# The delta rule's beta and alpha projection: which operand is stationary, in a two-block mixer kernel

## The chip, the cores and the metric

The kernel runs on one NeuronCore of a Trainium2 chip. The metric is the device time of one execution in microseconds; the figure given for a kernel is the median of several executions. TensorE (PE in the profile) multiplies; its weight loads are shown apart as PEld. VectorE is DVE, ScalarE is ACT, GpSimd is POOL, and SP issues the DMAs.

## The reference, cut to what matters

Two blocks of two layers each run over 256 tokens of width 1024. In each layer of the first block one input projection feeds a delta rule and a Hyena branch. Sixteen of its columns are the delta rule's beta logits and alpha:

```
proj = _rmsnorm(x, mix_norm[i]) @ w_in[i]
q, k, v, z, beta_logit, alpha, hy_in = jnp.split(proj, IN_SPLITS, axis=-1)
...
beta = jax.nn.sigmoid(beta_logit...)          # 8 columns: 2 directions x 4 heads
g = -jnp.exp(a_log) * jax.nn.softplus(alpha + dt_bias)   # 8 columns
o_fwd = _gated_delta_rule(q, k, v, beta[0], g[0])
```

So for these the kernel needs a 256 x 1024 by 1024 x 16 product in each of two layers. The kernel uses it with tokens on the partitions: two blocks of 128 tokens (`rb`), 16 columns each, 32 columns in all, in `small[:, 304:336]`.

## The kernel before

All weights of the two blocks are streamed from HBM in the order of use. SP loads 1 MB units into `raw`; ACT rounds each half (128 x 1024) to `w_hi` (L568), POOL takes the rest as `w_lo` (L949), and PE uses the pair. Each matrix product is three matmuls, in `product` (lines 412 to 414): low by high, high by low, high by high. There are four slots for halves; ACT works three halves ahead of PE.

`project_T(0, l, 66 + i, psA[:, i % 3, 0:L])` makes one block of 128 output channels by 256 tokens: over 8 blocks of the 1024 inputs (`kc`) it loads 128 x 128 weights as the stationary operand and moves `xT` (128 x 256), 24 matmuls in all. The text calls it project(i). In `stack1_projections` PE runs i from 0 to 27: 0 to 11 are Hyena's channels, 12 to 23 are q, k and v, and 24 to 27 are z. ACT takes each result out of PSUM (L719 for q, k, v), DVE adds the other four taps of the short convolution (`convolve1`, L1168, conv(i)), and ACT applies silu. Before project(i) PE waits for conv(i - 3), whose PSUM bank it takes. Between these steps stand, by a fixed list of i in each engine's own program, other pieces: on PE after i = 16 `gate_columns`, the product for beta and alpha, and after i = 22 `qk_sums`. On DVE, after conv(17), the 32 columns are copied to `small` (L1219); after conv(19) come the inverse root of the Hyena norm (L962 to L974) and the scaling of `zz` (L1225), after conv(20) the sums with alpha (L1230, L1232) which ACT turns into exponentials (L740) at i = 22.

In `gate_columns` the stationary operand is a 128 x 128 block of `xT`, and the 16 weight columns move: 2 blocks of tokens x 8 `kc` x 3 = 48 matmuls in a layer, each 128 x 16. In the profile's rows a matmul's names are given as output<-moving,stationary, so these read `psA<-wba_hi,xT_lo 128x16`, and those of project(i) read `psA<-xT_hi,w_lo 128x256`.

Each engine runs its own instructions strictly in the order written; semaphores of the table `s1` (`ba_mm`, `ba_out`, `conv`, and others) hold one engine for another.

Of the kernel before, what the change touches and what calls it, by code (L numbers as in the profile page):

```python
# [31 lines left out]
P = 128  # L32
D = 1024
L = 256
RB = L // P
KC = D // P
# [139 lines left out]
def emit(nc, ins, out, count):  # L176

    steps = {}
    with ExitStack() as ctx:
# [3 lines left out]
        def sb(name, shape, dt=F32):  # L183
            return ctx.enter_context(nc.sbuf_tensor(name, shape, dt))

        def psum(name, shape):
            return ctx.enter_context(nc.psum_tensor(name, shape, F32))
# [6 lines left out]
        xT_hi = sb("xT_hi", [P, KC, L], F32R)  # L194
        xT_lo = sb("xT_lo", [P, KC, L], F32R)
# [11 lines left out]
        small = sb("small", [P, 400])  # L207
        root_mix = sb("root_mix", [P, 2, L])
        ident, ones, blockones = mats[:, 0, :], mats[:, 1, :], mats[:, 2, :]
# [18 lines left out]
        def at(name, kb, shape, dt=F32):  # L228
            n = 4 * int(np.prod(shape[1:]))
            assert kb * KB + n <= ARENA, name  # L230
            return nc.alloc_sbuf_tensor_at(name, shape, dt, offset=at0 + int(kb * KB))
# [28 lines left out]
        hdn = at("hdn", 105.0, [HID, L + 1])  # L260
        farg = at("farg", 102.0, [HID, 2, L])
        skip = at("skip", 83, [P, 2, HYW])
        zz = at("zz", 103, [P, RB, HYW])
        knat = at("knat", 75, [P, RB, HEADS, P])
        vnat = at("vnat", 79, [P, RB, HEADS, P])
# [24 lines left out]
        wba_hi = at("wba_hi", 62, [P, KC, 16], F32R)  # L290
        wba_lo = at("wba_lo", 62.5, [P, KC, 16], F32R)
# [29 lines left out]
        psA = psum("psA", [P, 4, 512])  # L321
# [49 lines left out]
        def one_stack(per):  # L371
            return {k: Signal(sem(k), n) for k, n in per.items()}

        NPAR1, NPAR2 = 20, 14
        s1 = one_stack(dict(
            cols_tp=1, cols=1, wba=1, mlp_mm=3, mlp_arg=3, mlp_sin=3, filt_mm=8, filt=8, even=4, odd=4, spec_mm=10, spec=10,
            conv_mid=24, conv=24, qkv_silu=12, z_out=4, z_silu=1, ba_mm=1, ba_out=1, hy_turned=6, hy_nat=6,
            z_mm=8, y_spec=4, inv_mm=4, zz=4, hy_ss=2, hy_zn=1, hy_back=2, y_hi=6, y_lo=6,
            qk_sq=1, qk_mm=1, qk_root=1, qk_norm=1, kv_turned=4, kv_nat=4,
            g_arg=1, g_exp=1, g_sum=1, g_ln=1, g_ready=1, g_cum=1, g_col=1, g_decays=1,  # L380
            row_mm=4, row_arg=4, row_exp=4, q_exp=2, q_dec=2, kk_mm=1, attn=4, mt=5,
            masked=24, p_mm=28, q_new=24, t_new=4, u_new=4, tu_mm=20, tu_copy=24,
            v1_mm=2, v1=2, k_dec=2, s_mm=2, s_copy=2, ks_mm=2, rest=2, v2_mm=2, v2=2, o_mm=2,
# [26 lines left out]
        def product(o, a_hi, a_lo, b_hi, b_lo, start, stop, skip=False):  # L410

            nc.tensor.matmul(o, a_lo, b_hi, start=start, stop=False, skip_group_check=skip)  # L412
            nc.tensor.matmul(o, a_hi, b_lo, start=False, stop=False, skip_group_check=skip)  # L413
            return nc.tensor.matmul(o, a_hi, b_hi, start=False, stop=stop, skip_group_check=skip)  # L414
# [541 lines left out]
        def _(dve):  # L956
            V = nc.vector
# [249 lines left out]
            def stack1_projections(l):  # L1207
                ch = dve_chain[0]
                for i in range(24):
                    convolve1(l, i)  # L1210
                    if i in (10, 13):
                        spectral_product(l, i // 13, 0)
                        spectral_product(l, i // 13, 1)
                    if i in (12, 15):
                        hyena_gate(l, i // 15, 0)
                        hyena_gate(l, i // 15, 1)
                    if i == 17:
                        dve.wait_ge(s1["ba_mm"].sem, s1["ba_mm"].due(l, 1))
                        V.tensor_copy(small[:, 304:336], psA[:, 3, 0:32]).then_inc(s1["ba_out"].sem, 1)  # L1219
                        dve.wait_ge(s1["ba_out"].sem, s1["ba_out"].due(l, 1))  # L1220
                    if i == 19:
                        dve.wait_ge(s1["hy_ss"].sem, s1["hy_ss"].due(l, 2))
                        inverse_root(l, ch, small[:, 292:294], small[:, 288:290], 1.0 / HYW)
                        for rb in range(RB):
                            ins_ = V.tensor_scalar(zz[:, rb, :], zz[:, rb, :], small[:, 292 + rb:293 + rb], None, ALU.mult)  # L1225
                        ins_.then_inc(s1["hy_zn"].sem, 1)
                    if i == 20:
                        for rb in range(RB):
                            alpha = small[:, 312 + 16 * rb:320 + 16 * rb]
                            V.tensor_tensor(small[:, 16 + 8 * rb:24 + 8 * rb], alpha, small[:, 8:16], ALU.add).then_inc(ch.sem, 1)  # L1230
                            dve.wait_ge(ch.sem, ch.step(l))
                        V.scalar_tensor_tensor(small[:, 32:48], small[:, 16:32], -1.0, small[:, 16:32], ALU.mult, ALU.max)\  # L1232
                            .then_inc(s1["g_arg"].sem, 1)
# [318 lines left out]
            for col, value in ((eps, EPS), (eps64, 64 * EPS), (eps128, 128 * EPS), (stat[:, 3:4], D * EPS * EPS)):  # L1552
                ins_ = V.memset(col, value)
# [43 lines left out]
        def _(pe):  # L1597
# [31 lines left out]
            def project_T(st, l, s, o, q=None):  # L1629

                pe.wait_ge(lo_done[st].sem, lo_done[st].due(l, s + 1))
                hi, lo = split_half(w_hi, s, "A"), split_half(w_lo, s, "A")
                for kc in range(KC):
                    if q is not None and kc % 2 == 0:
                        pe.wait_ge(n_lo[st].sem, n_lo[st].due(l, 4 * q + kc // 2 + 1))
                    ins_ = product(o, hi[:, kc, :], lo[:, kc, :], xT_hi[:, kc, :], xT_lo[:, kc, :], kc == 0, kc == KC - 1)
                ins_.then_inc(half_used[st].sem, 1)
# [128 lines left out]
            def gate_columns(l):  # L1766

                pe.wait_ge(s1["wba"].sem, s1["wba"].due(l, 1))
                pe.wait_ge(s1["hy_nat"].sem, s1["hy_nat"].due(l, 6))
                for rb in range(RB):  # L1770
                    t = slice(rb * P, (rb + 1) * P)
                    for kc in range(KC):
                        ins_ = product(psA[:, 3, 16 * rb:16 * rb + 16], xT_hi[:, kc, t], xT_lo[:, kc, t],
                                       wba_hi[:, kc, :], wba_lo[:, kc, :], kc == 0, kc == KC - 1)
                ins_.then_inc(s1["ba_mm"].sem, 1)

            def qk_sums(l):
# [7 lines left out]
            def stack1_projections(l):  # L1785

                for i in range(28):
                    if 3 <= i < 27:
                        pe.wait_ge(s1["conv"].sem, s1["conv"].due(l, i - 2))
                    elif i == 27:  # L1790
                        pe.wait_ge(s1["z_out"].sem, s1["z_out"].due(l, 1))
                    project_T(0, l, 66 + i, psA[:, i % 3, 0:L], 1 if i == 0 else None)
                    if i == 5:
                        turn_hyena(l, 0)
                        turn_hyena(l, 1)
                    if i == 9:
                        turn_hyena(l, 2)
                        turn_hyena(l, 3)
                    if i == 10:
                        hyena_spectrum(l, 0)  # L1800
                    if i == 12:
                        hyena_inverse(l, 0)
                    if i == 13:
                        hyena_spectrum(l, 1)
                        turn_hyena(l, 4)
                    if i == 14:
                        turn_hyena(l, 5)
                    if i == 15:
                        hyena_inverse(l, 1)
                    if i == 16:  # L1810
                        gate_columns(l)
                    if i == 22:
                        qk_sums(l)
                pe.wait_ge(s1["hy_zn"].sem, s1["hy_zn"].due(l, 1))
                pe.wait_ge(s1["z_out"].sem, s1["z_out"].due(l, 2))
                pe.wait_ge(s1["ba_out"].sem, s1["ba_out"].due(l, 1))
                for b in range(4):
                    for rb in range(RB):
                        c = (b % 2) * L + rb * P
                        ins_ = nc.tensor.transpose(psA[:, 1 + b // 2 * 2, c:c + P], zz[:, rb, b * P:(b + 1) * P], ident)  # L1820
                    if b % 2:
                        ins_.then_inc(s1["hy_back"].sem, 1)
# [318 lines left out]
```

## Time and profile before

| | |
|---|---|
| median of 3 runs | 2204.73 us (2200.49 to 2206.77) |
| the profiled execution: its own time | 2204.25 us |
| its span in the trace | 2202.4 us |
| PE matmul busy | 2082.2 us, 95% |
| DVE, ACT, POOL busy | 974.9, 1033.1, 1496.3 us |
| mean granted TensorE clock | 0.977 of full |

A busy PE is an engine with a matmul under way, whatever clock it was granted and however few columns it moves. The granted clock is given as a share of full speed in the column PEclk of a table by stretches: 1.00 is 2.4 GHz and 0.50 is 1.2 GHz, and a value between them means that the stretch holds some of each. For the pace of a stream of matmuls the distance between two starts is to be read, not the duration of one, since they overlap.

### The profile page before, as it was taken

What the parts mean: (1) busy time and instruction counts of PE and PEld (TensorE: products, weight loads), DVE (VectorE), ACT (ScalarE), POOL (GpSimd) and SP (SyncE); (2) the same over time, 40 slices, a digit from 0 to 9 for tenths busy, and PEclk for the clock granted to TensorE, in tenths of its full rate; (3) what the DMA queues carried; (4) which work ended last, traced back from release to release, by engine and by line L of the source; (5) the groups of instructions that cost most, each with busy time, mean ns of one, the idle gap of its engine ahead of it and who ended that gap; (6) DMA issues with size and microseconds to landing.
All of it is one profiled execution on the core that took longest, in us unless ns stands there. A gap on an engine that the chain in (4) does not pass through costs nothing.

```text
span 2202.4 us, 37209 instructions
## 1 busy us (share of the span) xinstructions
PE 2082.2 (95%) x15887; PEld 1895.2 (86%) x15887; DVE 974.9 (44%) x1647; ACT 1033.1 (47%) x1532; POOL 1496.3 (68%) x656
## 2 busy tenths in 40 slices
PE   7999998899999999998899999889999998889999
PEld 6997768879989997778889988888899888888997
DVE  3550475524204551366533204555477026454760
ACT  5443426355446443516364436346644363366442
POOL 6788434238887887424258887657688866577886
PEclk9999998899999999998999999999999999999999
DMA  6756222025555655323025564444455544444553
GB/s 227 219 182 199 85 88 97 21 63 187 191 185 168 217 183 178 104 70 115 3 94 176 191 223 148 153 126 156 150 174 189 196 135 154 131 157 154 180 185 133
DMA packets 250397, 329.63 MB, mean 150 GB/s; under 512 B 9016, under 2 KB 224954, under 8 KB 249722
## 3 DMA queue, kind: packets, MB, share of 16 engines
q1 hardware_dynamic: 249834, 325.15, 45.7%
q8 instruction: 126, 2.06, 0.4%
q0 software_dynamic: 400, 2.10, 0.2%
q14 instruction: 37, 0.30, 0.0%
HBM read 326.18 MB, written 1.05 MB: 149 GB/s over the span
## 4 chain that ended last, share of the span: by engine, by line
PE 53%; DVE 6%; ACT 3%; POOL 2%; issue 1%; DVEq 0%; ACTq 0%
PE psA L412 11%; PE psA L413 10%; PE psA L414 10%; PE psB L412 5%; PE psB L413 5%; PE psB L414 5%; POOL w_lo L949 2%; PE psA L1733 1%; PE psB L1756 1%; PE psB L1763 1%; ACT w_hi L568 1%; DVE yacc L1536 0%; PE psA L1889 0%; PE psA L1891 0%; PE psB L1879 0%
## 5 line engine op out<-in xcount | busy, mean ns | idle before, releaser
L949 POOL TENSOR_TENSOR w_lo<-raw,w_hi 128x1024 fp32r<-128x1024 f32 x600 | 1461.9, 2454 | 634.2 <-ACT w_hi L568 631.8
L412 PE MATMUL psA<-xT_hi,w_lo 128*128 128x256 f32 x3296 | 955.3, 290 | 53.0 <-DVE xT_lo L999 15.4
L413 PE MATMUL psA<-xT_lo,w_hi 128*128 128x256 f32 x3296 | 941.2, 286 | 0.0
L414 PE MATMUL psA<-xT_hi,w_hi 128*128 128x256 f32 x3296 | 940.7, 285 | 0.0
L568 ACT ACTIVATE w_hi<-raw 128x1024 fp32r<-128x1024 f32 x600 | 628.8, 1051 | 409.6 <-PE psB L414 249.1
L412 PEld LDWEIGHTS psA<-xT_hi,w_lo 128*128 128x128 f32 x3296 | 641.2, 195 | 67.2 <-issue 25.9
L413 PEld LDWEIGHTS psA<-xT_lo,w_hi 128*128 128x128 f32 x3296 | 641.5, 195 | 3.0 <-issue 2.9
L414 PEld LDWEIGHTS psA<-xT_hi,w_hi 128*128 128x128 f32 x3296 | 641.2, 195 | 0.0
L1097 DVE TENSOR_TENSOR hT_lo<-hfull,hT_hi 128x256 fp32r<-128x256 f32 x132 | 220.4, 1701 | 2.3 <-ACT hT_hi L688 1.3
L413 PE MATMUL psB<-w_lo,hT_hi 128*128 128x512 f32 x528 | 209.5, 397 | 0.0
L412 PE MATMUL psB<-w_hi,hT_lo 128*128 128x512 f32 x528 | 209.0, 396 | 0.4 <-issue 0.4
L414 PE MATMUL psB<-w_hi,hT_hi 128*128 128x512 f32 x528 | 207.4, 393 | 0.0
L1041 DVE SCALAR_TENSOR_TENSOR x<-psB,stat,x 128x512 f32<-128x512 f32 x24 | 17.1, 752 | 336.5 <-PE psB L414 336.5
L1093 DVE TENSOR_TENSOR hfull<-sg,psA 128x256 f32<-128x256 f32 x132 | 55.0, 420 | 232.0 <-PE psA L414 219.0
L412 PEld LDWEIGHTS psB<-w_hi,hT_lo 128*128 128x128 f32 x528 | 99.1, 188 | 25.2 <-issue 0.8
L414 PEld LDWEIGHTS psB<-w_hi,hT_hi 128*128 128x128 f32 x528 | 99.1, 188 | 24.6
L413 PEld LDWEIGHTS psB<-w_lo,hT_hi 128*128 128x128 f32 x528 | 99.1, 188 | 22.7
L688 ACT ACTIVATE hT_hi<-hfull 128x256 fp32r<-128x256 f32 x132 | 54.4, 414 | 118.9 <-DVE hfull L1093 118.8
L679 ACT ACTIVATE sg<-gs 128x256 f32<-128x256 f32 x88 | 36.0, 413 | 147.3 <-DVE gs L1073 147.3
L1073 DVE TENSOR_TENSOR gs<-psA,root_row 128x256 f32<-128x256 f32 x88 | 35.8, 419 | 102.2 <-PE psA L414 73.6
L682 ACT ACTIVATE sg<-gconv 128x256 f32<-128x256 f32 x44 | 18.4, 417 | 100.9 <-DVE gconv L1060 100.9
L1168 DVE SCALAR_TENSOR_TENSOR qkvT<-psA,cols,qkvT 128x254 f32<-128x254 f32 (+1 forms) x96 | 46.1, 482 | 40.3 <-ACT qkvT L719 37.7
(415 smaller groups left out, 2257.6 us busy)
## 6 DMA issues: line engine op xcount, KB each, us to landing
raw<-in_w_in SPq DMA_DIRECT2D x78, 1024.0 KB, 5.3
raw<-in_ffn_w_gate SPq DMA_DIRECT2D x44, 1024.0 KB, 5.3
raw<-in_ffn_w_up SPq DMA_DIRECT2D x44, 1024.0 KB, 5.4
raw<-in_ffn_w_down SPq DMA_DIRECT2D x44, 1024.0 KB, 4.9
raw<-in_w_ffn_in SPq DMA_DIRECT2D x44, 1024.0 KB, 5.1
raw<-in_w_ffn_out SPq DMA_DIRECT2D x22, 1024.0 KB, 4.8
raw<-in_w_out SPq DMA_DIRECT2D x16, 1024.0 KB, 4.9
raw<-in_w_branch_da SPq DMA_DIRECT2D x4, 1024.0 KB, 4.9
```

The lines of the kernel that those rows point to most:

```text
L412: nc.tensor.matmul(o, a_lo, b_hi, start=start, stop=False, skip_group_check=skip)
L413: nc.tensor.matmul(o, a_hi, b_lo, start=False, stop=False, skip_group_check=skip)
L414: return nc.tensor.matmul(o, a_hi, b_hi, start=False, stop=stop, skip_group_check=skip)
L568: A(split_half(w_hi, n, kinds[n]), raw_half(n, kinds[n]), ACT.Copy).then_inc(hi_done[st].sem, 1)
L679: A(sg[:, i, :], gs[:, i, :], ACT.Silu).then_inc(f_act[st].sem, 1)
L688: A(hT_hi[:, n, :], hfull[:, i, :], ACT.Copy).then_inc(f_hi[st].sem, 1)
L949: nc.gpsimd.tensor_tensor(split_half(w_lo, n, kind), raw_half(n, kind), split_half(w_hi, n, kind).bitcast(F32), ALU.subtract)\
L1073: V.tensor_tensor(gs[:, i, :], psA[:, i, 0:L], root_row[:, :], ALU.mult).then_inc(f_gate[st].sem, 1)
L1093: V.tensor_tensor(hfull[:, i, :], sg[:, i, :], psA[:, 2 + i, 0:L], ALU.mult).then_inc(f_prod[st].sem, 1)
L1097: V.tensor_tensor(hT_lo[:, n, :], hfull[:, i, :], hT_hi[:, n, :].bitcast(F32), ALU.subtract)\
L1168: ins_ = V.scalar_tensor_tensor(o[:, a:z], ps[:, a + t:z + t], w[t + len(w) // 2], o[:, a:z], ALU.mult, ALU.add)
L1733: ins_ = M(psA[:, k % 4, :], dft_f[:, rb, b, :], src, start=(rb == 0), stop=(rb == RB - 1))
```

## The change

The operands of the product for beta and alpha change places. The 16 weight columns become the stationary operand and `xT` (128 x 256, all tokens at once) moves: 8 `kc` x 3 = 24 matmuls, whose result lies in PSUM as 16 partitions x 256 tokens. DVE copies it to a new SBUF tile `ba_row` (16 x 256) after conv(17). A new function `turn_gates` on PE, after project(18), waits for that copy and turns it by two transposes (matmuls with the unit matrix) into 128 x 16 each, beside the first result in the same PSUM bank. DVE copies the 32 columns to `small` after conv(19), where it did so after conv(17). `ba_mm` and `ba_out` are raised twice in a layer.

```
-            conv_mid=24, conv=24, ..., ba_mm=1, ba_out=1, ...
+            conv_mid=24, conv=24, ..., ba_mm=2, ba_out=2, ...
...
                     if i == 17:
                         dve.wait_ge(s1["ba_mm"].sem, s1["ba_mm"].due(l, 1))
-                        V.tensor_copy(small[:, 304:336], psA[:, 3, 0:32]).then_inc(s1["ba_out"].sem, 1)
-                        dve.wait_ge(s1["ba_out"].sem, s1["ba_out"].due(l, 1))
+                        V.tensor_copy(ba_row[:, :], psA[0:16, 3, 0:L]).then_inc(s1["ba_out"].sem, 1)
+                    if i == 19:
+                        dve.wait_ge(s1["ba_mm"].sem, s1["ba_mm"].due(l, 2))
+                        V.tensor_copy(small[:, 304:336], psA[:, 3, L:L + 32]).then_inc(s1["ba_out"].sem, 1)
+                        dve.wait_ge(s1["ba_out"].sem, s1["ba_out"].due(l, 2))
...
                 pe.wait_ge(s1["hy_nat"].sem, s1["hy_nat"].due(l, 6))
+                for kc in range(KC):
+                    ins_ = product(psA[0:16, 3, 0:L], wba_hi[:, kc, :], wba_lo[:, kc, :], xT_hi[:, kc, :], xT_lo[:, kc, :],
+                                   kc == 0, kc == KC - 1)
+                ins_.then_inc(s1["ba_mm"].sem, 1)
+
+            def turn_gates(l):
+
+                pe.wait_ge(s1["ba_out"].sem, s1["ba_out"].due(l, 1))
                 for rb in range(RB):
-                    t = slice(rb * P, (rb + 1) * P)
-                    for kc in range(KC):
-                        ins_ = product(psA[:, 3, 16 * rb:16 * rb + 16], xT_hi[:, kc, t], xT_lo[:, kc, t],
-                                       wba_hi[:, kc, :], wba_lo[:, kc, :], kc == 0, kc == KC - 1)
+                    ins_ = nc.tensor.transpose(psA[:, 3, L + 16 * rb:L + 16 * rb + 16], ba_row[:, rb * P:(rb + 1) * P], ident[0:16, 0:16])
                 ins_.then_inc(s1["ba_mm"].sem, 1)
...
                     if i == 16:
                         gate_columns(l)
+                    if i == 18:
+                        turn_gates(l)
```

The order of PE's instructions at the end of project(16) and the start of `gate_columns` in layer 0, in the kernel before (semaphores waited for in brackets):

```order
L413 MATMUL psA<-xT_lo,w_hi 128x256
L414 MATMUL psA<-xT_hi,w_hi 128x256
L412 MATMUL psA<-wba_hi,xT_lo 128x16 [waits hy_nat,wba]
L413 MATMUL psA<-wba_lo,xT_hi 128x16
L414 MATMUL psA<-wba_hi,xT_hi 128x16
```

The same place in the changed kernel, whose lines stand one further down:

```order
L414 MATMUL psA<-xT_lo,w_hi 128x256
L415 MATMUL psA<-xT_hi,w_hi 128x256
L413 MATMUL psA<-xT_hi,wba_lo 16x256 [waits hy_nat,wba]
L414 MATMUL psA<-xT_lo,wba_hi 16x256
L415 MATMUL psA<-xT_hi,wba_hi 16x256
```

Sixteen such triples have become eight, of 256 moving columns each where there were 16; project(17) follows directly in both. PE's order between project(18) and project(19) in the changed kernel, where the kernel before has nothing:

```order
L414 MATMUL psA<-xT_lo,w_hi 128x256
L415 MATMUL psA<-xT_hi,w_hi 128x256
L1783 MATMUL psA<-mats,ba_row 128x16 [waits ba_out]
L1783 MATMUL psA<-mats,ba_row 128x16
L413 MATMUL psA<-xT_hi,w_lo 128x256 [waits lo_done,conv]
L414 MATMUL psA<-xT_lo,w_hi 128x256
```

The two transposes stand behind a wait for DVE, and project(19) behind them. DVE's order from the end of conv(17) to the inverse root in the changed kernel:

```order
L1169 SCALAR_TENSOR_TENSOR qkvT<-psA,cols,qkvT 128x254 [waits dve_chain]
L1220 COPY ba_row<-psA 16x256 [waits ba_mm]
L1169 SCALAR_TENSOR_TENSOR qkvT<-psA,cols,qkvT 128x254 [waits conv_mid]
L1169 SCALAR_TENSOR_TENSOR qkvT<-psA,cols,qkvT 128x255 [waits dve_chain] x2
L1169 SCALAR_TENSOR_TENSOR qkvT<-psA,cols,qkvT 128x254 [waits dve_chain]
L1169 SCALAR_TENSOR_TENSOR qkvT<-psA,cols,qkvT 128x254 [waits conv_mid]
L1169 SCALAR_TENSOR_TENSOR qkvT<-psA,cols,qkvT 128x255 [waits dve_chain] x2
L1169 SCALAR_TENSOR_TENSOR qkvT<-psA,cols,qkvT 128x254 [waits dve_chain]
L1223 COPY small<-psA 128x32 [waits ba_mm]
L963 TENSOR_SCALAR stat<-small 128x2 [waits hy_ss,ba_out]
```

In the kernel before the one copy stands after conv(17):

```order
L1168 SCALAR_TENSOR_TENSOR qkvT<-psA,cols,qkvT 128x254 [waits dve_chain]
L1219 COPY small<-psA 128x32 [waits ba_mm]
L1168 SCALAR_TENSOR_TENSOR qkvT<-psA,cols,qkvT 128x254 [waits conv_mid,ba_out]
L1168 SCALAR_TENSOR_TENSOR qkvT<-psA,cols,qkvT 128x255 [waits dve_chain] x2
L1168 SCALAR_TENSOR_TENSOR qkvT<-psA,cols,qkvT 128x254 [waits dve_chain]
```

The copy of the 32 columns has moved behind conv(18) and conv(19), directly ahead of the inverse root, and the copy of the 16 x 256 row has taken its old place.

## Rows read from the trace of the kernel before

**Rows 1.** The page: busy time of the engines, share of the span.

```profile
PE 2082.2 (95%) x15887; PEld 1895.2 (86%) x15887; DVE 974.9 (44%) x1647; ACT 1033.1 (47%) x1532; POOL 1496.3 (68%) x656
```

**Rows 2.** Timeline of PE, layer 0 (start us, duration us, engine, line).

```profile
326.01 0.26 PE L413 MATMUL psA<-wba_lo,xT_hi 128*128 128x16 f32 x1
326.12 0.26 PE L414 MATMUL psA<-wba_hi,xT_hi 128*128 128x16 f32 x1
...
329.13 0.36 PE L413 MATMUL psA<-wba_lo,xT_hi 128*128 128x16 f32 x1
329.35 0.36 PE L414 MATMUL psA<-wba_hi,xT_hi 128*128 128x16 f32 x1
```

**Rows 3.** Busy time by stretch, layer 0.

```profile
core 0: us, PE busy (x) PEld busy (x) DVE busy (x) ACT busy (x) POOL busy (x), PEclk, DMA share, GB/s
325.86:328.92 3.06, 3.06 (x31) 3.06 (x29) 1.93 (x4) 1.72 (x3) 0.94 (x1) 1.00 0.01 2
328.92:333.33 4.41, 4.41 (x23) 4.41 (x22) 0.00 (x0) 0.00 (x0) 1.41 (x1) 0.50 0.02 4
333.33:338.47 5.14, 5.14 (x26) 5.14 (x26) 0.00 (x0) 0.00 (x0) 0.00 (x0) 0.50 0.00 0
338.47:341.70 3.23, 3.23 (x26) 3.23 (x26) 2.03 (x5) 1.73 (x3) 0.99 (x1) 0.89 0.00 0
```

**Rows 4.** Busy time by stretch, layer 1, the columns as before.

```profile
981.62:984.22 2.60, 2.60 (x26) 2.60 (x25) 1.78 (x4) 1.72 (x3) 0.60 (x1) 1.00 0.00 0
984.22:989.31 5.09, 5.09 (x26) 5.09 (x26) 0.15 (x1) 0.00 (x0) 1.76 (x1) 0.51 0.00 0
989.31:994.40 5.09, 5.09 (x25) 5.09 (x26) 0.00 (x0) 0.00 (x0) 0.00 (x0) 0.50 0.00 0
994.40:997.40 3.00, 3.00 (x26) 3.00 (x26) 2.03 (x5) 1.73 (x3) 0.84 (x1) 0.98 0.03 5
```

**Rows 5.** Timeline of DVE, layer 0 (in brackets: idle before, who ended it).

```profile
339.41 2.04 DVE L1168 SCALAR_TENSOR_TENSOR qkvT<-psA,cols,qkvT 128x254 f32<-128x254 f32 x4 [10.69 <-ACT qkvT L719]
341.37 0.18 DVE L1219 COPY small<-psA 128x32 f32<-128x32 f32 x1
342.53 2.04 DVE L1168 SCALAR_TENSOR_TENSOR qkvT<-psA,cols,qkvT 128x254 f32<-128x254 f32 x4 [0.98 <-ACT qkvT L719]
345.34 2.04 DVE L1168 SCALAR_TENSOR_TENSOR qkvT<-psA,cols,qkvT 128x254 f32<-128x254 f32 x4 [0.78 <-ACT qkvT L719]
347.29 0.16 DVE L962 TENSOR_SCALAR stat<-small 128x2 f32<-128x2 f32 x1
...
356.83 2.02 DVE L1168 SCALAR_TENSOR_TENSOR qkvT<-psA,cols,qkvT 128x254 f32<-128x254 f32 x4
```

**Rows 6.** Timeline of PE's weight loads, layer 0.

```profile
358.91 0.19 PEld L412 LDWEIGHTS psA<-xT_hi,w_lo 128*128 128x128 f32 x1 [2.87 <-DVE qkvT L1168]
```

**Rows 7.** Busy time by stretch, and the page's group of a 64-column matmul.

```profile
414.00:432.00 18.00, 18.00 (x624) 18.00 (x622) 6.12 (x16) 9.39 (x14) 4.90 (x8) 1.00 0.02 4
L1889 PE MATMUL psA<-Q,TU 64*64 64x64 f32 x640 | 40.6, 226 | 0.1
```

**Rows 8.** Timeline of ACT, layer 0.

```profile
338.90 0.47 ACT L719 ACTIVATE qkvT<-psA,cols 128x256 f32<-128x256 f32 x1 [11.00 <-PE psA L414]
```

**Rows 9.** The page's group of a 128x256 DVE operation that reads PSUM.

```profile
L1073 DVE TENSOR_TENSOR gs<-psA,root_row 128x256 f32<-128x256 f32 x88 | 35.8, 419 | 102.2 <-PE psA L414 73.6
```

**Rows 10.** Timeline of PE, layer 0: four transposes, and the second product matmul after.

```profile
312.91 0.63 PE L1744 MATMUL psA<-mats,hyT 128*128 128x128 f32 x4 [1.14 <-ACT hynat L724]
...
313.49 0.28 PE L413 MATMUL psA<-xT_lo,w_hi 128*128 128x256 f32 x1
313.61 0.28 PE L414 MATMUL psA<-xT_hi,w_hi 128*128 128x256 f32 x1
```

**Rows 11.** Timeline of POOL, layer 0.

```profile
340.71 2.42 POOL L949 TENSOR_TENSOR w_lo<-raw,w_hi 128x1024 fp32r<-128x1024 f32 x1 [10.38 <-ACT w_hi L568]
```

**Rows 12.** Timeline of PE, layer 0: 512-column matmuls on unrounded tiles.

```profile
319.67 3.60 PE L1763 MATMUL psB<-Ysp,dft 128*128 128x512 f32 x8
```

More of the change, by code:

```diff
@@ L262, in emit @@
         skip = at("skip", 83, [P, 2, HYW])
+        ba_row = at("ba_row", 102, [16, L])
         zz = at("zz", 103, [P, RB, HYW])
@@ L376, in emit @@
             cols_tp=1, cols=1, wba=1, mlp_mm=3, mlp_arg=3, mlp_sin=3, filt_mm=8, filt=8, even=4, odd=4, spec_mm=10, spec=10,
-            conv_mid=24, conv=24, qkv_silu=12, z_out=4, z_silu=1, ba_mm=1, ba_out=1, hy_turned=6, hy_nat=6,
+            conv_mid=24, conv=24, qkv_silu=12, z_out=4, z_silu=1, ba_mm=2, ba_out=2, hy_turned=6, hy_nat=6,
             z_mm=8, y_spec=4, inv_mm=4, zz=4, hy_ss=2, hy_zn=1, hy_back=2, y_hi=6, y_lo=6,
@@ L1815, in stack1_projections @@
                 pe.wait_ge(s1["z_out"].sem, s1["z_out"].due(l, 2))
-                pe.wait_ge(s1["ba_out"].sem, s1["ba_out"].due(l, 1))
+                pe.wait_ge(s1["ba_out"].sem, s1["ba_out"].due(l, 2))
                 for b in range(4):
```

## The prediction, made blind

> **What bounds the kernel now.** I read the page first, then the part of PE's timeline in which the changed product lies, then the same stretch as a table with the granted clock, and last DVE's timeline behind it. The page says that PE is busy for 2082.2 us, 95% of the span [rows 1]: what PE is spared counts, unless another engine sets the pace where it is spared. It doesn't say how well PE uses the time, and the stretch shows that it uses it badly.
>
> The 48 matmuls of 16 columns start 0.11 us apart at first (326.01, 326.12) and 0.22 us apart later (329.13, 329.35) [rows 2]. A project(i) moves 256 columns in each matmul, and two of these start 0.12 us apart at full clock (313.49, 313.61) [rows 10]. So moving 16 columns takes as long as moving 256; with so few to move, the load of a 128-column stationary block must be what sets the 0.11 us. The doubling is the clock: it is 1.00 in the first 3.06 us of the block, then 0.50 for the other 4.41 us, though PE is busy in all of it, and 0.50 still in all 5.14 us of project(17); project(18) has 0.89 [rows 3]. Layer 1 repeats it: 2.60 us at 1.00, 5.09 at 0.51, project(17) 5.09 at 0.50, project(18) 3.00 at 0.98 [rows 4]. Twice the clock falls from 2.4 to 1.2 GHz some 3 us into a stretch in which PE moves 16 columns every 0.11 us, and comes back only after the 256-column matmuls have run for over 5 us.
>
> Who waits for PE there? DVE sat idle 10.69 us ahead of conv(17), 0.98 ahead of conv(18) and 0.78 ahead of conv(19), each time for ACT, which waited for PE (ACT's own row: 11.00 us) [rows 5, 8]. From conv(19) on DVE is the one that sets the pace: its inverse root starts at 347.29 as conv(19) ends, it has no idle bracket up to conv(20) at 356.83, and PE's next weight load waits 2.87 us for that [rows 5, 6]. So the path runs PE, project(17) to (19), then DVE from conv(19), then PE again. What PE gains up to project(19) passes whole to conv(19) and to all behind it; what is added to DVE between conv(19) and conv(20) is paid in full.
>
> **The change part by part.**
>
> Removed: the 16-column matmuls. Layer 0 takes from the block's start to the start of project(19) 3.06 + 4.41 + 5.14 + 3.23 = 15.84 us [rows 3]; layer 1 takes 2.60 + 5.09 + 5.09 + 3.00 = 15.78 us [rows 4].
>
> Put in their place: 24 matmuls of 256 columns with a 16-column stationary block. No row shows this shape. From below, nothing says that it is slower than the same moving operand with a 128-column stationary block, 0.12 us [rows 10]. From above, the 512-column matmuls on unrounded tiles take 3.60 / 8 = 0.45 us [rows 12], so 0.225 us for 256 columns. I take 0.12, since both operands are the rounded tiles that project(i) uses. That is 24 x 0.12 = 2.88 us. The Trainium skill (TensorE: Matmul & The Clock Gate, section LDWEIGHTS) has a weight load take as many cycles of 1.2 GHz as it has columns, which is 107 ns for 128 columns, near the measured 0.11 us, and an estimated 13 ns for 16. By that page only the 256 columns would be left, 109 ns by its gap formula; the block would be an estimated 24 x 0.109 = 2.6 us and the whole 0.5 us shorter over two layers.
>
> The clock: the block now moves columns at the pace of project(i), so I expect 1.00 throughout it. Narrow stationary blocks alone are no reason for a fall: at 414 to 432 us PE runs 624 matmuls, mostly 64 x 64 on a 64-column block, in 18.00 us (29 ns each) at 1.00 [rows 7]. Then project(17) and project(18) cost 24 x 0.12 = 2.88 us each, and the way to project(19) is 3 x 2.88 = 8.64 us, without the new wait. Gain: 15.84 - 8.64 = 7.20 us and 15.78 - 8.64 = 7.14 us.
>
> Added on PE, `turn_gates`. Everything behind it on PE (project(19) onward) waits with it for DVE's copy of `ba_row`. In layer 0, project(17) ended at 338.47 [rows 3], ACT took it out from 338.90 [rows 8], conv(17) ran from 339.41 and the copy followed at 341.37 [rows 5], which is 2.90 us after the end of project(17). At full clock the last matmul drains some 0.1 us sooner (0.28 us long where it was 0.41), so 2.8. The copy took 0.18 us for 32 columns [rows 5]; for 256 columns the nearest row is a DVE operation of that width from PSUM, 0.419 us [rows 9], which I take: partitions are fewer, columns are the same. It is ready at 2.8 + 0.42 = 3.22 us, and PE is through with project(18) at 2.88: a stall of 0.35 us, between 0.1 (a copy of 0.18) and 0.6. Then two transposes. Four of them and the first product matmul behind take 313.49 - 312.91 = 0.58 us [rows 10], less 0.12 for the product is 0.46, so 0.24 for two. Sum 0.6 us a layer, bounds 0.3 to 0.9. The wait for the copy's own sake costs DVE nothing: conv(18) had 0.98 us of idle time ahead of it [rows 5], more than the 0.42; were that cover gone, 0.4 us.
>
> Added on DVE's path: the copy of 32 columns now stands between conv(19) and the inverse root, where nothing covers it; 0.18 us and its release, 0.2 us a layer. At its old place it was covered, so nothing comes back. The transposes are long done by then (conv(19) follows project(19), which follows them).
>
> Untouched: the weights. POOL's w_lo of the half for project(21) ran from 340.71 to 343.13 [rows 11]; it is released by the end of project(17), so it moves forward with it, and PE wants it only three projects after that. DMA is all but idle in the stretch (share 0.00 to 0.03) [rows 3, 4].
>
> Sum: layer 0 7.20 - 0.6 - 0.2 = 6.4 us, layer 1 7.14 - 0.8 = 6.34 us, together 12.7 us. The profiled execution took 2204.25 us, its span included; it becomes 2191.5. The median of the runs lies 0.5 us above it, 2204.73, so the forecast is **2192.0 us**, 0.58% faster. Of the 12.7 us less than half comes from the smaller count of matmuls at equal clock (48 x 0.11 = 5.3 against 2.88, 2.4 us a layer); the rest is the clock.
>
> **The rivals.**
>
> *The clock falls all the same.* In both layers the fall came 2.6 to 3.1 us after the block began [rows 3, 4], about the 2.88 us that the new block lasts. If the cause were something else than the few moving columns (the 16 wide stationary block feeds an eighth of the array; or what ran before the block), the clock would fall at its end and project(17) with a piece of project(18) run at half: (5.14 - 2.88) + (3.23 - 2.88) = 2.6 us a layer lost again. 12.7 - 5.2 = 7.5 us, 2197.2 us. The row of 64-column blocks at 1.00 [rows 7] speaks against it, and so does the doubling in a stretch of tiny moves. The Trainium skill (TensorE: Matmul & The Clock Gate, section Why this matters for your kernels) asks only that PE have no long idle gaps to stay at full clock; by that rule a PE busy without a gap could not have lost its clock here, the fall would have a cause that the change leaves alone, and the time would be that of this rival. The trace disagrees: busy 4.41 of 4.41 us at 0.50 [rows 3]. Chance 0.13.
>
> *The gain is not passed on*: something that the trace hides behind PE (a release on ACT, a half of weights) holds project(17) to (19) or conv(19) at their old distance, and at most half arrives: 2198.5 to 2204.7 us. For it speaks only that such things are common; against it, that DVE and ACT were idle for PE for over 10 us [rows 5, 8]. Chance 0.04.
>
> *Slower: the new shape runs in the slow form.* If the matmuls with a 16-column block ran like those on unrounded tiles and brought the clock down as well, each would take 0.45 us: 10.8 us for the block, 5.14 and 3.23 behind it, 19.2 us where it was 15.8, and 0.8 for the turning. That is 4.2 us a layer, 2213 us. It decides from (15.8 - 0.8 - 5.14 - 3.23) / 24 = 0.28 us a matmul with the half clock behind it, or 0.38 with the full clock. At 0.225 the kernel is still faster. The tiles are the rounded ones, hence 0.03.
>
> **How the numbers follow.** Forecast 0.80, the clock 0.13, not passed on 0.04, slow form 0.03. No change is what lies within 0.3%, 6.6 us, about what a measurement of this kernel can tell. The forecast's own range is 2188.5 to 2195.5: the turning at its bounds (0.6 us), and a fall of the clock elsewhere, in the stretches where PE waits for DVE, coming or going with the shift, some 2.5 us. The first rival's 7.5 us lies just beyond 6.6: I count 0.08 of its 0.13 as faster. Faster 0.80 + 0.08 = 0.88, same 0.05 + 0.04 = 0.09, slower 0.03. The range reaches to the first rival and leaves out the others: 2187.5 to 2198.5.
>
> **What would show it.** In the changed profile: 24 matmuls of the block 0.12 us apart; granted clock 1.00 from there through project(18); project(17) and (18) 2.9 us each; a PE wait for DVE's `ba_row` of some 0.35 us ahead of the transposes; DVE's idle time ahead of conv(17) down from 10.7 to about 4 us; a DVE copy of 0.18 us between conv(19) and the inverse root; and PE's wait for conv(20) still near 2.9 us. It is wrong if PEclk falls to 0.50 at project(17), if the block's matmuls are 0.2 us apart or more, or if these steps are right and the layer behind them has not moved forward by 6.4 us.

## The result, and the profile after

The changed kernel takes 2189.07 us (median of 5 runs, 2184.49 to 2193.24), the kernel before 2204.22 us in the same measurement (5 runs, 2200.49 to 2206.77). The ratio is 0.9935, 95% interval 0.9922 to 0.9948: faster by 15.2 us, with the interval at 11.5 to 17.2 us. Forecast were 12.7 us and 2192.0, range 2187.5 to 2198.5. A second measurement of the unaltered changed kernel gave 2188.87 us and 0.9925 (0.9912 to 0.9938).

The page of the changed kernel, beside [rows 1]:

```profile
span 2187.2 us, 37123 instructions
PE 2067.9 (95%) x15843; PEld 1879.3 (86%) x15843; DVE 972.5 (44%) x1649; ACT 1034.9 (47%) x1532; POOL 1497.5 (68%) x656
```

PE's busy share is still 95%; the share could not show what was wrong, nor that it is mended. The table by stretches does: block, project(17), and project(18) with the turning, in layer 0 and then the turning's stretch in layer 1 (the columns are those of [rows 3]; the third from the end is the granted clock).

```profile
326.03:328.80 2.77, 2.77 (x27) 2.28 (x25) 1.93 (x4) 1.73 (x3) 0.77 (x1) 1.00 0.00 0
328.80:331.67 2.87, 2.87 (x26) 2.87 (x25) 0.00 (x0) 0.00 (x0) 1.63 (x1) 1.00 0.02 6
331.67:335.01 3.34, 3.26 (x28) 3.03 (x26) 2.25 (x5) 1.99 (x4) 1.33 (x1) 1.00 0.00 0
...
978.31:981.65 3.34, 3.26 (x28) 3.03 (x26) 2.25 (x5) 1.99 (x4) 1.33 (x1) 1.00 0.00 0
```

The clock stays at 1.00. The way from the first matmul of the block to the first of project(19) is 2.77 + 2.87 + 3.34 = 8.98 us, where it was 15.77 and 15.80. (The 15.84 of [rows 3] starts at 325.86 us, one matmul of project(16) too early, and ends at 341.70, just before project(19) starts at 341.75.) PE's timeline at the turning, PE's weight loads at its two waits for DVE, and DVE's timeline, layer 0:

```profile
326.03 0.28 PE L413 MATMUL psA<-xT_hi,wba_lo 128*16 128x256 f32 x1
326.14 0.28 PE L414 MATMUL psA<-xT_lo,wba_hi 128*16 128x256 f32 x1
326.26 0.28 PE L415 MATMUL psA<-xT_hi,wba_hi 128*16 128x256 f32 x1
...
334.43 0.28 PE L415 MATMUL psA<-xT_hi,w_hi 128*128 128x256 f32 x1
334.79 0.29 PE L1783 MATMUL psA<-mats,ba_row 16*128 16x16 f32 x2
335.01 0.39 PE L413 MATMUL psA<-xT_hi,w_lo 128*128 128x256 f32 x1
335.24 0.28 PE L414 MATMUL psA<-xT_lo,w_hi 128*128 128x256 f32 x1
```

```profile
334.79 0.20 PEld L1783 LDWEIGHTS psA<-mats,ba_row 16*128 16x128 f32 x2 [0.28 <-DVE ba_row L1220]
...
352.08 0.19 PEld L413 LDWEIGHTS psA<-xT_hi,w_lo 128*128 128x128 f32 x1 [2.68 <-DVE qkvT L1169]
```

```profile
332.38 2.04 DVE L1169 SCALAR_TENSOR_TENSOR qkvT<-psA,cols,qkvT 128x254 f32<-128x254 f32 x4 [3.60 <-ACT qkvT L720]
334.33 0.40 DVE L1220 COPY ba_row<-psA 16x256 f32<-16x256 f32 x1
335.25 2.04 DVE L1169 SCALAR_TENSOR_TENSOR qkvT<-psA,cols,qkvT 128x254 f32<-128x254 f32 x4 [0.52 <-ACT qkvT L720]
338.69 2.04 DVE L1169 SCALAR_TENSOR_TENSOR qkvT<-psA,cols,qkvT 128x254 f32<-128x254 f32 x4 [1.40 <-ACT qkvT L720]
340.64 0.18 DVE L1223 COPY small<-psA 128x32 f32<-128x32 f32 x1
340.86 1.72 DVE L963 TENSOR_SCALAR stat<-small 128x2 f32<-128x2 f32 x1
342.62 0.17 DVE L965 TENSOR_SCALAR small<-stat 128x2 int32<-128x2 int32 x1
342.82 0.17 DVE L967 TENSOR_SCALAR small<-small 128x2 int32<-128x2 int32 x1
342.90 2.41 DVE L968 TENSOR_SCALAR stat<-stat 128x2 f32<-128x2 f32 x1
...
347.11 2.97 DVE L1229 TENSOR_SCALAR zz<-zz,small 128x512 f32<-128x512 f32 x2
350.00 2.02 DVE L1169 SCALAR_TENSOR_TENSOR qkvT<-psA,cols,qkvT 128x254 f32<-128x254 f32 x4
```

DVE's idle time ahead of conv(17) is down to 3.60 us from 10.69 [rows 5]. Without the turning the next matmul after project(18) would have started at 334.55. The transposes start at 334.79, after DVE's copy, and the first matmul of project(19) at 335.01, 0.46 us late. Its second matmul comes 0.23 us after the first, not 0.12, so the turning costs another 0.11 us behind that point, 0.57 in all. The copy of 32 columns stands bare between conv(19) and the inverse root and moves it by 0.22 us. Ahead of project(23) PE waits 2.68 us for conv(20), where it waited 2.87 [rows 6].

Two things that I had taken as fixed changed too. Two steps of DVE's inverse root take 1.72 and 2.41 us here, where the others take 0.16 to 0.17; [rows 5] left out the long ones of the kernel before. And the clock behind conv(20) is another.

### The profile page after: what moved, and what is told of

It reads as the page before. It is cut to its first block, busy times and chain, and to the rows that moved or that the text cites. A ratio compares the mean times of both kernels' runs of the same rounds, so it can differ in the third digit from the quotient of the medians.

```text
span 2187.2 us, 37123 instructions
## 1 busy us (share of the span) xinstructions
PE 2067.9 (95%) x15843; PEld 1879.3 (86%) x15843; DVE 972.5 (44%) x1649; ACT 1034.9 (47%) x1532; POOL 1497.5 (68%) x656
## 4 chain that ended last, share of the span: by engine, by line
PE 53%; DVE 6%; ACT 3%; POOL 2%; issue 1%; DVEq 0%; ACTq 0%
PE psA L413 11%; PE psA L414 10%; PE psA L415 10%; PE psB L413 5%; PE psB L414 5%; PE psB L415 5%; POOL w_lo L950 2%; PE psA L1737 1%; PE psB L1760 1%; PE psB L1767 1%; ACT w_hi L569 1%; DVE yacc L1540 0%; PE psA L1900 0%; PE psA L1902 0%; PE psB L1890 0%
## 5 line engine op out<-in xcount | busy, mean ns | idle before, releaser
L1480 DVE TENSOR_TENSOR gates<-psA,root_mix 128x256 f32<-128x256 f32 x48 | 20.1, 422 | 84.3 <-PE psA L415 84.3
```

## The experiments

**One alteration to the kernel before: 128 moving columns instead of 16.**

```
+                rep = lambda w: w.unsqueeze(1).to_broadcast([P, 8, 16])
...
-                        ins_ = product(psA[:, 3, 16 * rb:16 * rb + 16], xT_hi[:, kc, t], xT_lo[:, kc, t],
-                                       wba_hi[:, kc, :], wba_lo[:, kc, :], kc == 0, kc == KC - 1)
+                        ins_ = product(o, xT_hi[:, kc, t], xT_lo[:, kc, t],      # o: 128 columns
+                                       rep(wba_hi[:, kc, :]), rep(wba_lo[:, kc, :]), kc == 0, kc == KC - 1)
```

DVE's copy takes the 32 columns from their new places; it stays where it was. The mark `...` stands for lines of the code that are left out.

> The kernel before, with one thing altered: each of the 48 matmuls moves its 16 weight columns eight times over (128 columns in a row, seven eighths of them a repetition that nobody reads). Same count of matmuls, same 128-column stationary blocks, same order. Theory (few moving columns bring the clock down): 48 matmuls 0.11 us apart, granted clock 1.00 in the block and in project(17) and (18); the way to project(19) is 5.3 + 2.9 + 2.9 = 11.1 us instead of 15.8, so some 9.5 to 11 us faster than before, 2193 to 2195. Rival (the clock falls for a cause that the moving operand has no part in): it falls to 0.50 as before, 2204, no change.

Measured: 2194.01 us, ratio to before 0.9952 (0.9940 to 0.9964), 10.9 us faster with eight times the multiplications. Block, project(17) and project(18), layer 0:

```profile
325.79:331.10 5.31, 5.31 (x50) 5.31 (x49) 1.93 (x4) 1.73 (x3) 2.37 (x1) 1.00 0.01 3
331.10:334.03 2.93, 2.93 (x26) 2.93 (x26) 0.00 (x0) 0.00 (x0) 0.00 (x0) 1.00 0.00 0
334.03:336.91 2.88, 2.88 (x26) 2.88 (x25) 2.03 (x5) 1.73 (x3) 0.87 (x1) 1.00 0.00 0
```

There are 48 weight loads and 48 matmuls as before, and each pair takes 0.11 us, as it did with 16 columns while the clock was at 1.00 [rows 2]. Here the clock stays. So the fall hangs on the columns moved, and beside the load of a 128-column stationary block 128 moving columns cost no more than 16.

**The same with 64 columns** (repeated four times).

> As the kernel before with each of the 48 matmuls moving its 16 columns four times over (64 columns). If moving columns decide, this lies between 16 (clock 0.50 after some 3 us) and 128: either 1.00 throughout and 2193 to 2195, or a fall as before and 2204. Rival that the moving operand has no part in it: as before, 2204.

Measured: 2203.11 us, ratio 0.9997 (0.9985 to 1.0008): no change. The block in layer 0, then the block and project(17) in layer 1:

```profile
325.34:332.65 7.31, 7.31 (x50) 7.31 (x49) 1.93 (x4) 1.72 (x3) 2.36 (x1) 0.71 0.01 2
977.68:982.96 5.28, 5.28 (x51) 5.28 (x49) 1.93 (x4) 1.72 (x3) 2.35 (x1) 1.00 0.00 0
982.96:987.42 4.46, 4.46 (x27) 4.46 (x26) 0.00 (x0) 0.00 (x0) 0.00 (x0) 0.62 0.00 0
```

With 64 columns every 0.11 us the clock falls too. In layer 0 it falls within the block. In layer 1 it falls only behind the block, some 0.7 us into project(17), and is at 0.51 from 983.70 to 987.20 us, although project(17) moves 256 columns in each matmul.

**The 16-column matmuls dealt out among those of project(17) and project(18).**

```
+                for kc in range(KC):
+                    ins_ = product(o, hi[:, kc, :], lo[:, kc, :], xT_hi[:, kc, :], xT_lo[:, kc, :], kc == 0, kc == KC - 1)
...
+                    ins_ = product(psA[:, 3, 16 * rb:16 * rb + 16], xT_hi[:, kc, t], xT_lo[:, kc, t],
+                                   wba_hi[:, kc, :], wba_lo[:, kc, :], kc == 0, kc == KC - 1)
```

DVE's copy of the 32 columns moves with it, from behind conv(17) to behind conv(18).

> The kernel before, with its 48 matmuls of 16 columns unaltered but dealt out among those of project(17) and project(18): after each three matmuls of 256 columns three of 16 (DVE's copy of the 32 columns moves from after conv(17) to after conv(18)). Theory (the clock falls where PE moves few columns for microseconds on end): 16-column matmuls between 256-column ones keep the clock at 1.00; project(17) and (18) take 24 x 0.12 + 24 x 0.11 = 5.5 us each, 11.1 us to project(19) instead of 15.8, 2193 to 2195. Rival (it is the 16-column matmuls as such, wherever they stand): the clock falls in project(17) or (18) and the time is 2200 to 2204.

Measured: 2193.30 us, ratio 0.9953 (0.9940 to 0.9966), 11.5 us faster than before with not one matmul fewer. The two mixed projects in layer 0:

```profile
326.53:332.10 5.57, 5.57 (x52) 5.57 (x50) 1.95 (x5) 2.10 (x5) 2.38 (x1) 1.00 0.01 3
332.10:337.70 5.60, 5.60 (x51) 5.60 (x50) 2.00 (x5) 1.79 (x4) 2.37 (x1) 1.00 0.10 25
```

The clock is 1.00 in both. The rival that such matmuls bring the clock down wherever they stand is refuted: they did it in a row of 48, and not three by three among wide ones.

**The changed kernel's block run twice**, `for kc in (*range(KC), *range(KC))`.

> The changed kernel, with its block of 24 matmuls run twice (the second pass overwrites the first with the same numbers): 48 matmuls of 256 moving columns on 16-column stationary blocks, 5.5 us. Theory: 0.115 us each, clock 1.00 throughout and behind it, so 2.77 us a layer or 5.5 us in all slower than the changed kernel: 2194 to 2195. Rival (a narrow stationary block counts as little work too, and the block of the changed kernel was only too short to show it): the clock falls to 0.50 in the second pass, project(17) runs at 0.213 us a matmul, 5 us a layer are lost besides: 2203 or more.

Measured: 2197.84 us (10 runs, 2191.33 to 2200.80), 3.4 us above the 2194.4 that two blocks more give, though its profile, the fastest of its runs, had the clock at 1.00 in the block:

```profile
325.75:331.30 5.55, 5.55 (x51) 4.53 (x49) 1.93 (x4) 1.73 (x3) 2.38 (x1) 1.00 0.01 4
331.30:334.17 2.87, 2.87 (x26) 2.87 (x25) 0.00 (x0) 0.00 (x0) 0.00 (x0) 1.00 0.00 0
```

So I ran **the block four times**, and later the twofold one once more.

> The changed kernel, with its block of 24 matmuls run four times (96 matmuls of 256 moving columns on 16-column stationary blocks, 11.1 us a layer; the last pass gives the result). Run twice, the block kept the clock at 1.00 in the profile, but its median was 3 us above the 2194.4 that 2 x 2.77 us more than the changed kernel give. Theory (only moving columns count): clock 1.00 in all 11.1 us, project(17) 2.9 us, 3 x 2.77 x 2 = 16.6 us above the changed kernel's 2189: 2205 to 2207. Rival (narrow stationary blocks bring the clock down after some time, in most executions later than 5.5 us): PEclk 0.50 in the later passes, 2212 or more.

Measured: 2204.14 us (10 runs, 2199.76 to 2207.58), 15.1 us above the changed kernel where 16.6 were expected, and just below the forecast of 2205 to 2207. Block and project(17), layer 0:

```profile
325.80:336.90 11.10, 11.10 (x99) 9.09 (x97) 1.93 (x4) 1.67 (x3) 2.39 (x1) 1.00 0.01 1
336.90:339.80 2.90, 2.90 (x27) 2.90 (x26) 0.00 (x0) 0.10 (x1) 0.00 (x0) 1.00 0.00 0
```

That is 11.1 us of nothing but 16-column stationary blocks, at 1.00 throughout. The rival that a narrow stationary block brings the clock down is refuted.

> The kernel with the block run twice, once more, unaltered. Its median was 2197.8 us where 2194.4 was expected, and the one profiled execution was its fastest (2191.3) and kept its clock in the block. Theory: the block keeps its clock again and takes 5.55 us a layer; a slower execution differs elsewhere, where PE waits. Rival: in the usual, slower execution the clock falls in the second pass of the block or in project(17) (8.4 us to project(18) becomes 9.5 or more in one of the layers).

Measured: 2193.60 us (5 runs, 2191.20 to 2198.78), as first expected (2194.4); the two medians of this kernel lie 4.2 us apart. This time the profiled execution was the slowest, 2198.78 us, and its block took 5.54 us in both layers and project(18) began at 8.41 and 8.42 us, as in the first profile. What makes one execution of a kernel 7 us slower than another is thus not in the block. The mean granted clock is 0.978 here and was 0.984 there, and this profile is at half clock in stretches where that one is at 1.00, such as 16.10 to 26.30, 463.20 to 470.00 and 1005.90 to 1009.30 us. Ahead of each of these three PE had stood idle for part of the time; that the idle time brought the fall is not shown.

**The changed kernel once more, and the kernel before twice more,** unaltered.

> The changed kernel once more, unaltered, for a second profile and times on the chip of its variants. The stretch from the block to conv(20) should repeat within 0.1 us. What lies behind it in layer 0 (there the first profile had gained 1.5 us more than up to conv(20)) repeats if it belongs to the change, and differs if it is the chance of where the clock falls while PE waits for DVE. Time 2185 to 2193.

> The kernel before once more, unaltered, for a second profile. The block, project(17) and (18) should repeat: clock 0.50 from some 3 us into the block to the start of project(18), 15.8 us to project(19), in both layers. The fall of the clock at 360 to 363 us in layer 0, which the changed kernel didn't show, repeats if it belongs to the kernel.

> The kernel before a third time, for two more layers' worth of the clock's fall. Theory: in both layers the clock falls some 2.5 to 3.1 us into the block and comes back 6 to 10.3 us later; between conv(20) and the end of conv(23) some layers have a second fall (9.45 us instead of 8.5), which none of the kernels that keep their clock in the block had in 8 of 9 cases.

Measured: 2188.87 us (5 runs) for the changed kernel; one run each, 2204.52 and 2207.30, for the kernel before. The steps, counted from the first matmul of the block, in us (worked out from the timelines; each column gives the start of its piece. The memset is DVE's of `U` behind conv(23), L1241, in the changed kernel L1245, and the last step is the time from conv(20) to it):

| profile, layer | project(19) | inverse root | conv(20) | memset | last step |
|---|---|---|---|---|---|
| before, 0 | 15.8 | 21.3 | 30.9 | 40.3 | 9.4 |
| before, 1 | 15.8 | 21.3 | 30.9 | 40.3 | 9.5 |
| second profile of before, 0 | 14.3 | 19.8 | 29.3 | 37.8 | 8.5 |
| second profile of before, 1 | 15.8 | 21.3 | 30.9 | 40.3 | 9.5 |
| third profile of before, 0 | 14.2 | 19.7 | 29.3 | 38.7 | 9.4 |
| third profile of before, 1 | 15.8 | 21.4 | 30.9 | 40.4 | 9.5 |
| changed, 0 | 9.0 | 14.8 | 24.0 | 32.5 | 8.5 |
| changed, 1 | 9.0 | 14.8 | 24.0 | 33.4 | 9.5 |
| second profile of changed, 0 and 1 | 9.0 | 14.8 | 24.0 | 32.5 | 8.5 |

The changed kernel repeats to 0.1 us up to conv(20); the kernel before doesn't, though I had expected 15.8 us to project(19) in all its layers. In the third profile of before, layer 0, the fall came 4.5 us into the block and not some 3 (block from 326.59 on, then its end and project(17)); in layer 1 it came after 2.3 us (980.79 to 983.10 at 1.00, 983.10 to 993.30 at 0.50).

```profile
326.59:331.20 4.61, 4.61 (x44) 4.61 (x43) 1.93 (x4) 1.72 (x3) 2.35 (x1) 0.99 0.01 4
331.20:337.80 6.60, 6.60 (x32) 6.60 (x32) 0.00 (x0) 0.00 (x0) 0.00 (x0) 0.50 0.00 0
```

In layer 0 the half clock lasted some 7 us, and as long in layer 0 of the second profile; in the four other layers it lasted some 10. The last step has two values. Where it takes 8.5 us, the clock is at 1.00. Where it takes 9.4 or 9.5, the clock has fallen once more after PE's wait for conv(20), as these two rows show, the first of the kernel before and the second of the changed one at the same place:

```profile
360.00:361.00 1.00, 1.00 (x6) 1.00 (x6) 0.93 (x3) 0.74 (x1) 0.19 (x1) 0.50 0.55 221
```

```profile
353.00:354.00 1.00, 1.00 (x11) 1.00 (x10) 0.93 (x3) 0.92 (x1) 0.01 (x1) 1.00 0.93 381
```

Five of six layers of the kernel before have this second fall and one of four of the changed kernel. The kernels that keep their clock in the block have it in 2 of 16 layers (the changed kernel, the one below, 128 columns, dealt out, twice, four times), those that lose it (the kernel before and the one with 64 columns) in 6 of 8. It is worth 0.95 us a layer. That it is bound up with the first fall is a count, not a mechanism.

**The turning brought forward.** The row is copied after conv(16), PE transposes after project(17), the 32 columns are copied after conv(17).

```
+                    if i == 16:
+                        dve.wait_ge(s1["ba_mm"].sem, s1["ba_mm"].due(l, 1))
+                        V.tensor_copy(ba_row[:, :], psA[0:16, 3, 0:L]).then_inc(s1["ba_out"].sem, 1)
                     if i == 17:
-                        V.tensor_copy(ba_row[:, :], psA[0:16, 3, 0:L]).then_inc(s1["ba_out"].sem, 1)
-                    if i == 19:
                         dve.wait_ge(s1["ba_mm"].sem, s1["ba_mm"].due(l, 2))
...
-                    if i == 18:
+                    if i == 17:
                         turn_gates(l)
```

> The changed kernel with the turning brought forward: DVE copies the 16 x 256 row after conv(16), in its idle time ahead of conv(17), PE transposes after project(17), and the 32 columns are copied after conv(17). Theory: PE's wait for the row (0.3 us a layer) and the copy of 0.2 us between conv(19) and the inverse root go away and nothing takes their place: 0.5 us a layer, 1.0 us in all, 2188 against 2189 of the changed kernel, to be seen in the trace and hardly in the times. Rival: the turning costs nothing on the path anyway, no difference in the stretch from the block to conv(20).

Measured: 2189.67 us (2186.62 to 2192.60), 0.9932 (0.9920 to 0.9944): no gain, where 1.0 us was expected. The trace says why. Up to the inverse root it is 0.36 us ahead in both layers (14.47 us after the block's start, not 14.83), and at conv(20) it is level (24.01, not 23.97). DVE's timeline of this kernel, and POOL's:

```profile
341.22 0.16 DVE L963 TENSOR_SCALAR stat<-small 128x2 f32<-128x2 f32 x1
341.41 2.31 DVE L965 TENSOR_SCALAR small<-stat 128x2 int32<-128x2 int32 x1
343.76 2.34 DVE L967 TENSOR_SCALAR small<-small 128x2 int32<-128x2 int32 x1
346.02 0.15 DVE L968 TENSOR_SCALAR stat<-stat 128x2 f32<-128x2 f32 x1
```

```profile
338.91 7.17 POOL L950 TENSOR_TENSOR w_lo<-raw,w_hi 128x1024 fp32r<-128x1024 f32 x3 [2.11 <-ACT w_hi L569]
```

Three w_lo of POOL follow one another from 338.91 to 346.08, each 2.4 us. DVE's two long steps end within 0.03 us of the second and the third (343.72 and 346.10 against 343.70 and 346.08). Which steps are long depends on when they come: here L965 and L967, in the changed kernel L963 and L968. What arrives earlier waits longer: the root takes 6.75 us here and 6.25 in the changed kernel.

**The inverse root's values in PSUM**, so that none of its instructions has two SBUF inputs or goes from SBUF to SBUF (the order of two multiplications is exchanged for that, y x v x y for y x y x v).

```
+                pv, pz, py, pd = psA[:, 3, 320:322], psA[:, 3, 322:324], psA[:, 3, 324:326], psA[:, 3, 326:328]
+                V.tensor_scalar(pv, total, scale, EPS, ALU.mult, ALU.add).then_inc(ch.sem, 1)
...
+                    V.tensor_tensor(pz, dst, pv, ALU.mult).then_inc(ch.sem, 1)
...
+                    V.tensor_tensor(py, pz, dst, ALU.mult).then_inc(ch.sem, 1)
...
+                    V.scalar_tensor_tensor(dst, py, 1.5, dst, ALU.add, ALU.mult).then_inc(ch.sem, 1)
```

> The changed kernel, with one thing altered behind the change: the intermediate values of the Hyena norm's inverse root (2 columns each) lie in PSUM instead of SBUF, so that no instruction of it has two SBUF inputs or reads and writes SBUF alone. In all profiles so far one or two of its 0.16 us instructions took 1.7 to 2.4 us and ended as a POOL w_lo ended. Theory (DVE waits there for the SBUF port that it shares with POOL): from conv(19)'s end to the scaling of zz 12 steps of 0.2 us, 2.5 us, where it was 6.3; conv(20) comes 3.8 us earlier, PE's wait of 2.7 us before project(23) all but disappears; 2.7 us a layer or so, 2183 to 2186. Rival (the long ones are the instructions' own, of integers): they stay at 2 us and the time at 2189.

Measured: 2182.51 us (5 runs, 2181.87 to 2183.19), 0.9908 (0.9894 to 0.9922), 6.4 to 6.6 us faster than the changed kernel's two medians and a little better than the forecast of 2183 to 2186. DVE's root, and the weight load at which PE waited 2.68 us:

```profile
341.80 0.16 DVE L981 TENSOR_SCALAR psA<-small 128x2 f32<-128x2 f32 x1
341.99 0.17 DVE L983 TENSOR_SCALAR psA<-psA 128x2 int32<-128x2 int32 x1
342.20 0.16 DVE L985 TENSOR_SCALAR small<-psA 128x2 int32<-128x2 int32 x1
342.27 0.16 DVE L986 TENSOR_SCALAR psA<-psA 128x2 f32<-128x2 f32 x1
...
344.25 2.64 DVE L1247 TENSOR_SCALAR zz<-zz,small 128x512 f32<-128x512 f32 x2
```

```profile
350.57 0.19 PEld L413 LDWEIGHTS psA<-xT_hi,w_lo 128*128 128x128 f32 x1 [0.24 <-issue]
```

The root takes 2.45 us (341.80 to 344.25), where it took 6.25 (340.86 to 347.11), with POOL at work in 2.13 of them. PE no longer waits for DVE ahead of project(23). The operations, their sizes and POOL's work are as they were; where the values lie is new. The rival that the long steps are the integer instructions' own is refuted: those take 0.17 us.

The wait has not left DVE altogether. The scaling of `zz` behind the root still reads and writes SBUF; its first instruction takes 2.24 us here and 0.49 in the changed kernel, and it ends 0.3 us after POOL's w_lo (343.81 to 346.21).

**Both together.**

> Both alterations of the changed kernel together: the inverse root's values in PSUM, and the turning brought forward (row copied after conv(16), transposes after project(17), the 32 columns copied after conv(17)). Alone, bringing it forward shortened the way to the inverse root by 0.36 us and DVE lost it again in the root to a longer wait for POOL. Theory: without that wait the 0.36 us stay, 0.7 us less than the kernel with the PSUM root alone; 2182 to 2185. Rival: PE is the one that sets the pace to project(23) by then, and its way to project(19) is only 0.05 us shorter: no difference between the two.

Measured: 2181.85 us (2180.07 to 2184.31), 0.9906 (0.9892 to 0.9920). The median is 0.66 us below that of the PSUM root alone, but the runs of the two overlap, so no difference can be told. In the trace the theory fails: the root starts 0.37 us earlier, and conv(20) comes at 19.92 us against 19.86, since the two instructions on `zz` take 3.08 us and not 2.64, the first of them again until POOL's w_lo is through. The rival fits better: PE sets the pace to project(23), with a way to project(19) of 8.93 us against 8.98, and the memset comes 0.17 us earlier (29.84 us against 30.01).

## Why the prediction was right, and where its sum was short

The direction, the mechanism and the place were right; the time lies inside the range, though the range would also have held the first rival's 2197.2 us, and it is the profile that tells the two apart. Step by step:

- **The fall of the clock comes of few moving columns.** Shown from three sides: more moving columns in the same 48 matmuls keep the clock (128) or don't (64); the same 16-column matmuls in other company keep it; four blocks of narrow stationary operands in a row keep it. The first rival, with a chance of 0.13, is refuted.
- **24 matmuls at 0.12 us, 2.88 us.** They took 2.77, 0.115 us each. The gain is 0.1 us a layer more than the sum had.
- **The turning, 0.6 us.** Measured: 8.98 less 2.77 and twice 2.87 is 0.47 us up to project(19), and with the 0.11 us behind its first matmul nearly 0.6. The total came out right because two of its terms missed in opposite ways: PE's stall was 0.24 us where the sum had 0.35, and the transposes with the start behind them cost 0.33 where it had 0.24. The sum counted the copy from the end of project(17) at 338.47 us, which is a matmul early; project(18) starts at 338.66. The copy itself took 0.40 us, as estimated from the row of an operation of the same width (0.419).
- **The copy between conv(19) and the inverse root, 0.2 us.** 0.22.
- **The gain passes whole to DVE and on.** It did: 6.8 us at project(19) in both layers of the first pair of profiles, 6.5 at the inverse root, which is 13.0 us for two layers against the 12.7 of the sum. In two of six layers of the kernel before there were only 5.2 to 5.3 us to be had at project(19), since the half clock was shorter there.
- **From conv(19) DVE's work is what it was, and the weights are untouched.** This step was mis-sized. The root took 6.74 us in the kernel before (347.29 to 354.03), 6.25 in the changed one, since it meets POOL's w_lo at another moment: conv(20) came 0.4 us a layer sooner than the sum had it. I had read the absence of idle brackets there as work; some 4 us of it are waiting, as the 2.45 us of the root in PSUM show. The two long steps of the kernel before in layer 0, and POOL's three w_lo beside them:

```profile
347.49 2.31 DVE L964 TENSOR_SCALAR small<-stat 128x2 int32<-128x2 int32 x1
349.83 2.34 DVE L966 TENSOR_SCALAR small<-small 128x2 int32<-128x2 int32 x1
```

```profile
344.98 7.15 POOL L949 TENSOR_TENSOR w_lo<-raw,w_hi 128x1024 fp32r<-128x1024 f32 x3 [1.86 <-ACT w_hi L568]
```

- **A fall of the clock elsewhere, some 2.5 us either way.** It came out on the gaining side: 0.95 us in most layers.

The sum for a layer in which both happen: 6.8 at project(19), less 0.1 for the rest of the turning and 0.2 for the copy (6.5 at the root), plus 0.4 at conv(20) is 6.9, plus 0.95 at the memset is 7.8 us. In the first pair of profiles layer 0 gained 7.8 us, and layer 1, where the changed kernel has the second fall as well, 6.9: together 14.7 of the 15.2 us between the spans. That these profiles explain the measured gain so fully is in part luck. Averaged over all profiles of the table the two layers gain 13.8 us up to the memset, while the mean spans differ by 16.1; the other 2.3 us lie elsewhere and were not traced.

How the 15 us divide: 128 columns at equal count took away 10.9 us (interval 7.9 to 13.2), so some two thirds are the clock. The remaining 4 to 5 us are the 24 matmuls fewer in a layer, less the turning, and the shorter root; conv(20) comes 26.2 us after the block's start with 128 columns and 24.0 in the changed kernel, in both layers.

Left open: why the second fall goes with the first, and why the fall comes 2.3 to 4.5 us into the block of the kernel before and lasts 7 us in some executions and 10 in others. No kernel with a width between 64 and 128 columns was run.

## What to carry to other kernels

Read the granted clock beside PE's busy time, stretch by stretch. A run of matmuls that move few columns each can be 100% busy, cost as much as if it moved eight times as many, and leave the wide matmuls behind it at half clock. Let the narrow operand be the stationary one. If the layout forbids that, deal the narrow matmuls out among wide ones, which alone gave 11.5 of the 15 us here without a transpose or a matmul fewer. And where an engine's tiny instructions take 2 us, look at what another engine ends at that moment, before you move the work behind them about.

## What the hardware showed that was not expected

- Matmuls on 128-column stationary blocks start 0.11 us apart with 16, 64 or 128 moving columns at full clock (48 of them take 5.28 us with 64 and 5.31 with 128). The clock fell with 16 and with 64, and not with 128.
- In every profile with the root in SBUF two of its two-column DVE instructions (0.16 us) took 1.7 to 2.4 us beside POOL's 2.4 us subtraction, and each ended within 0.04 us of the end of one. With a PSUM operand in each of them 13 in a row took 2.45 us beside a busy POOL. The Trainium skill has the rule (Advanced Engine Details and Errata, Mode Summary): the second SBUF port of VectorE is shared with GpSimd, and GpSimd's instructions and those of VectorE that use both ports block each other. The trace agrees, and adds the price: up to a whole POOL instruction each time, on the path, however small DVE's own is.
- Two executions of the twofold block, both with the clock at 1.00 in it, took 2191.33 and 2198.78 us; the medians of 10 and of 5 runs of that kernel lay 4.2 us apart.
